# GpSimd scales expert 0's output, constant products before the gathered rows, and a reordered, halved last weight split, in a decoder layer with hierarchical MoE

## The reference, cut to what matters

```python
def hier_moe(x, w_group, b_group, w_expert, b_expert, w_gate, w_up, w_down):
    xt = x.reshape(B_ * S, D)                       # 512 x 1024
    ...
    combine = jnp.einsum('tk,tke->te', w_tok, jax.nn.one_hot(gid, N_EXPERTS, dtype=jnp.float32)).astype(x.dtype)
    y = jnp.zeros_like(xt)
    for e in range(N_EXPERTS):                      # 16
        h = jax.nn.silu(xt @ w_gate[e]) * (xt @ w_up[e])
        y = y + combine[:, e:e + 1] * (h @ w_down[e])
    return y.reshape(B_, S, D)

def reference(...):
    ...
        x = layer_norm(DEEPNORM_ALPHA * x + mix, ln1_g[l], ln1_b[l])
        moe = hier_moe(x, w_group[l], b_group[l], w_expert[l], b_expert[l], w_gate[l], w_up[l], w_down[l])
        x = layer_norm(DEEPNORM_ALPHA * x + moe, ln2_g[l], ln2_b[l])
```

## Time and profile before

| | us |
|---|---|
| median of 3 runs (663.3 to 665.82) | 664.22 |
| the profiled execution | 664.12 |
| its span, first to last instruction | 662.3 |
| TensorE busy | 619.7 (94%) |
| VectorE busy | 479.0 (72%) |
| ScalarE busy | 377.3 (57%) |
| GpSimd busy | 100.5 (15%) |
| granted TensorE clock, mean | 0.971 |

### The profile page before, as it was taken

One profiled execution on the slowest core, in us unless ns is written; L12 is line 12 of the kernel. 1 busy time (PEld: TensorE's weight loads), 2 busy tenths in 40 slices (PEclk: granted clock), 3 DMA queues, 4 the chain that ended last, 5 costly groups with the idle time before them and its releaser, 6 DMA issues.

```text
span 662.3 us, 9787 instructions
## 1 busy us (share of the span) xinstructions
PE 619.7 (94%) x3745; PEld 499.6 (75%) x3745; DVE 479.0 (72%) x554; ACT 377.3 (57%) x401; POOL 100.5 (15%) x78
## 2 busy tenths in 40 slices
PE   9998999999999999999599599999999999999990
PEld 7877788787767888887477388888888888888870
DVE  3668698884357334455778478899898898888857
ACT  4568234531306576311555478777877777878734
POOL 0023124450000000000156111101111111110000
PEclk9999999999999999999889799999999999999995
DMA  8732131125006000956589889999999999999353
GB/s 332 246 129 95 54 109 64 64 71 133 2 1 190 1 1 2 389 245 254 192 329 421 277 301 388 391 392 390 393 391 390 392 392 401 401 403 380 85 156 127
DMA packets 42413, 155.25 MB, mean 234 GB/s; under 512 B 11923, under 2 KB 12131, under 8 KB 30092
## 3 DMA queue, kind: packets, MB, share of 16 engines
q1 hardware_dynamic: 37500, 138.40, 54.1%
q0 software_dynamic: 4880, 16.39, 9.5%
HBM read 139.96 MB, written 14.81 MB: 234 GB/s over the span
## 4 chain that ended last, share of the span: by engine, by line
PE 82%; DVE 5%; ACT 4%; issue 3%; DMA 3%; POOL 2%; DVEq 0%; ACTq 0%; POOLq 0%
PE psum L618 23%; PE psum L620 21%; PE psum L619 21%; PE psum L851 3%; PE psum L627 2%; PE psum L731 2%; PE psum L1001 2%; PE psum L1018 1%; DMA slot_dram<-rec_i,addr_i 1%; PE psum L829 1%; PE psum L842 1%; PE psum L761 1%; DMA slots<-slot_dram 1%; POOL slot_dram L553 1%; DVE ring L1462 1%
## 5 line engine op out<-in xcount | busy, mean ns | idle before, releaser
L1656 DVE TENSOR_TENSOR w_lo<-ring,w_hi 128x2048 fp32r<-128x2048 f32 x96 | 218.3, 2290 | 24.5 <-ACT w_hi L1282 24.2
L618 PE MATMUL psum<-w_hi,act_hi 128*128 128x512 f32 x544 | 222.2, 408 | 12.1 <-DVE w_lo L1656 8.3
L620 PE MATMUL psum<-w_hi,act_lo 128*128 128x512 f32 x544 | 214.1, 394 | 0.0
L619 PE MATMUL psum<-w_lo,act_hi 128*128 128x512 f32 x544 | 213.9, 393 | 0.0
L1282 ACT ACTIVATE w_hi<-ring 128x2048 fp32r<-128x2048 f32 x96 | 182.0, 1916 | 25.0 <-PE psum L620 25.0
L618 PEld LDWEIGHTS psum<-w_hi,act_hi 128*128 128x128 f32 x544 | 103.3, 190 | 40.1 <-issue 12.6
L620 PEld LDWEIGHTS psum<-w_hi,act_lo 128*128 128x128 f32 x544 | 103.0, 189 | 22.4
L619 PEld LDWEIGHTS psum<-w_lo,act_hi 128*128 128x128 f32 x544 | 103.4, 190 | 19.1
L1417 DVE TENSOR_TENSOR w_lo<-ring,w_hi 128x2048 fp32r<-128x2048 f32 x17 | 41.8, 2462 | 33.6 <-ACT w_hi L1131 33.4
L579 POOL DMA_INDIRECT acc_dram<-misc,slots x15 | 23.9, 1597 | 217.9 <-ACT misc L1332 217.9
L1131 ACT ACTIVATE w_hi<-ring 128x2048 fp32r<-128x2048 f32 x17 | 32.5, 1915 | 42.7 <-PE psum L620 41.0
(11 more groups left out here) (232 smaller groups left out, 723.3 us busy)
## 6 DMA issues: line engine op xcount, KB each, us to landing
ring<-in_w_gate SPq DMA_DIRECT2D x32, 1024.0 KB, 11.9
ring<-in_w_up SPq DMA_DIRECT2D x32, 1024.0 KB, 13.9
ring<-in_w_down SPq DMA_DIRECT2D x32, 1024.0 KB, 11.5
ring<-in_w_in SPq DMA_DIRECT2D x13, 1024.0 KB, 5.4
ring<-in_w_o SPq DMA_DIRECT2D x4, 1024.0 KB, 5.0
acc_dram<-ring SPq DMA_DIRECT2D x5, 512.0 KB, 3.6
ring<-in_x SPq DMA_DIRECT2D x2, 1024.0 KB, 6.4
ring<-strip_dram SPq DMA_DIRECT2D x8, 256.0 KB, 5.0
```

The costliest lines, as they stand in the source:

```text
L618: pe.matmul(dst, lh, rh, start=first, stop=False, skip_group_check=True)
L619: pe.matmul(dst, lh, rl, start=False, stop=False, skip_group_check=True)
L620: return pe.matmul(dst, ll, rh, start=False, stop=last, skip_group_check=True)
L1656: dve.tensor_tensor(w_lo[:, v0 % WBUF, :], ring[:, slot, :], w_hi[:, v0 % WBUF, :].bitcast(F32), ALU.subtract).then_inc(s_lo, 1)
```

## The change

Three parts. **Expert 0's output.** ScalarE copies it unscaled to `yb` as soon as its down product is complete (`first_out`), without waiting for a weight. GpSimd, once the table is there, multiplies these 128x1024 numbers by the weights in place, and then scatters them. `weight_column(0)` goes; the new product counts in its place, and expert 1's output waits for one count instead of two. **Constants.** TensorE issues 24 constant matmuls into bank 1 before it waits for the first gathered rows; before the last expert's down product it issues 6 and 10 instead of 24 and 14. **The last units.** VectorE makes the last expert's gated product before the low part of unit 95 and makes that low part in two halves, the low part of the turned product between them. TensorE waits for each half where it first needs it. The column and the one-hot rows of the last expert come behind all of this on VectorE.

```diff
-            weight_column(0)
             weight_column(1)
             pool.wait_ge(s_acc, 16 * (T + 1))
+            pool.wait_ge(s_y, 1)
+            pool.tensor_scalar(yb[:, 0, :], yb[:, 0, :], weight_of(slots[:, 0, 2:3]), None, ALU.mult).then_inc(s_wnow, 1)
+            pool.wait_ge(s_wnow, 2)
             for e in range(NE - 1):
...
+            keep_warm(24, 1)
             pe.wait_ge(s_xg[0], 16)
...
-            keep_warm(24, 0)
+            keep_warm(6, 0)
             transpose_h(NE)
-            keep_warm(14, 0)
+            keep_warm(10, 0)
             pe.wait_ge(s_htlo, NE)
             pe.wait_ge(s_y, NE - 1)
-            pe.wait_ge(s_lo, MIX_UNITS + 6 * NE)
+            pe.wait_ge(s_lo, MIX_UNITS + 6 * NE - 1)
             for dhalf in range(2):
                 for c in range(4):
+                    if dhalf == 0 and c >= 2:
+                        pe.wait_ge(s_lolast, c - 1)
...
-                act.wait_ge(s_wnow, e + 1)
+                act.wait_ge(s_wnow, 1 if first else e + 1)
                 act.activation(yb[:, b, :], banks(5, 2), ACT.Copy, scale=w_now[:, b:b + 1]).then_inc(s_y, 1)
+
+            def first_out(v0):
+
+                act.wait_ge(s_used, MIX_UNITS + v0)
+                act.activation(yb[:, 0, :], banks(5, 2), ACT.Copy).then_inc(s_y, 1)
...
-                y_out(s - 1, 1 - b, v + 4, j, first=s0 <= 2)
+                if s0 == 1:
+                    first_out(v + 4)
+                else:
+                    y_out(s - 1, 1 - b, v + 4, j, first=s0 == 2)
...
-                elo(v + 7, j)
+                if ahead:
+                    elo(v + 7, j)
                 hidden(s, v + 6, j)
...
+            def last_lo(part):
+
+                v0 = 6 * NE - 1
+                cols = slice(part * D, (part + 1) * D)
+                return dve.tensor_tensor(w_lo[:, v0 % WBUF, cols], ring[:, (v0 + 3) % RING, cols],
+                                         w_hi[:, v0 % WBUF, cols].bitcast(F32), ALU.subtract)
+
+            dve.wait_ge(s_hi, MIX_UNITS + 6 * NE)
+            dve.wait_ge(s_used, MIX_UNITS + 6 * NE - WBUF)
+            last_lo(0).then_inc(s_lolast, 1)
+            dve.wait_ge(s_hthi, NE)
+            dve.tensor_tensor(h_lo, bank(4), h_hi.bitcast(F32), ALU.subtract).then_inc(s_htlo, 1)
+            last_lo(1).then_inc(s_lolast, 1)
+            dve.wait_ge(s_lolast, 2)
+            dve.sem_inc(s_lo, 1)
             dve.wait_ge(s_flag, 2)
             over = dve.value_load(over_i[0:1, 0:1], min_val=0, max_val=1)
             dve.wait_ge(s_slotd, 16)
             link(dve.tensor_copy(last_row, slots[:, NE - 1, 1:2]))
             dve.wait_ge(s_lnw, 80)
             dve.tensor_scalar(hot_last, token_no, last_row, None, ALU.is_equal).then_inc(s_onehot, 1)
-            dve.wait_ge(s_hthi, NE)
-            dve.tensor_tensor(h_lo, bank(4), h_hi.bitcast(F32), ALU.subtract).then_inc(s_htlo, 1)
```

More of the change, by code:

```diff
@@ L325, in build @@
         s_comb, s_zsum, s_nmu, s_rstd = sem("s_comb"), sem("s_zsum"), sem("s_nmu"), sem("s_rstd")
-        s_xo = sem("s_xo")
+        s_xo, s_lolast = sem("s_xo"), sem("s_lolast")
         w_in = t["w_in"].rearrange("(k p) (b n) -> p k b n", p=P, n=WIDTH)
```

## The result

The changed kernel takes 655.43 us (median of 4 runs, 654.15 to 655.68), the kernel before 663.85 us (4 runs, 663.3 to 665.82): ratio 0.9867, 95% interval 0.985 to 0.9883. The forecast was 651.3 us with a range of 648.6 to 654.8, so the direction was right and the gain, 8.4 us, is two thirds of the 12.8 forecast. The profiled execution took 655.68 us, its span is 653.9.

A forecast was written before the change was run, and what follows sets the result against it. The expert loop was taken as TensorE's, with DMA engines as full, time being winnable only at three stops or slow-clock places; from 664.1 us, -10.7 + 1.0 + 0.3 - 1.6 - 1.8 = -12.8 gave 651.3 us, range 648.6 to 654.8.

The forecast's parts named there:

- Expert 0's output, -10.7: Second expert step: without ScalarE's wait for the weight column, TensorE's hole and its slow clock go, -10.7 us.
- The weights, nothing: Weight loads, needed up to 12.3 us earlier, keep about 4 us of reserve; costed at nothing.
- The rival of weights running dry: End of the loop: TensorE waits for weight loads and gives back up to 5 us, 656 us; chance 0.05.
- VectorE held by the product, +1.0 (0 to +2.2): GpSimd's product near 368 to 370 us holds a VectorE split; about half reaches TensorE, +1.0 us.
- The gather chain, +0.3 (0 to +3): GpSimd's queue from product through two scatters to expert 4's gather: rows at about 394.8, needed at 396; +0.3 us.
- my rival on the slow side: Gather chain's end: a product of 13.7 us or more, with low clock costing 2.5 us, makes a loss; chance 0.02.
- the gather chain is late: Expert 4's rows: scatter or product longer than assumed, 1 to 4 us more, 652.5 to 655.5 us; chance 0.10.
- The constants, -1.6 (+1.5 to -2.0): Router's end: 24 constant products before the first gathered rows bring the full clock back earlier, -1.6 us.
- near 331: Router's end: with the constants starting at 327.6, the full clock may be back near 331 us instead of 337.3.
- The tail, -1.8: Last expert: gated product starts 1.9 us earlier, the load of the sums holds 0.1 back; -1.8 us, bounds -1.9 and 0.
- that rival: Tail: with fewer constant products the clock falls, 24 down matmuls cost 5.3 us more, 656.6 us; chance 0.05.

The follow-up runs named there:

- the gather ahead: Changed kernel with GpSimd issuing expert 4's gather once the slot table is there, before the product and both scatters: 650.37 us, ratio 0.979.
- the half product: Changed kernel with GpSimd's product on only the first 512 of 1024 columns of expert 0's output: 654.47 us, ratio 0.9869.
- two products: Changed kernel with GpSimd's product on expert 0's output made twice, one after the other: 658.07 us, ratio 0.9914.
- the repeat of the better kernel: Changed kernel with expert 4's gather issued before the product and both scatters, run again unchanged in a later batch: 651.17 us, ratio 0.9801.
- all gathers ahead: Kernel with expert 4's gather before product and scatters, plus gathers of experts 5 to 7 before the wait for the preceding scatter: 649.4 us, ratio 0.9787.
- the old output: Changed kernel with expert 0's output waiting for its weight column again, no GpSimd product, constants and new tail kept: 660.43 us, ratio 0.995.

## Why the forecast was right in direction and wrong in size

**Expert 0's output, -10.7.** Measured -10.8. Taking the last step of the loop as the model for the undisturbed one held to 0.1 us.

**The weights, nothing.** No high part waited for a load, and the up units, from 320 us on, took 14.1 us to land in the median. The rival of weights running dry fell.

**VectorE held by the product, +1.0 (0 to +2.2).** 0 in the changed kernel; about 0.8 with the gather ahead, where the step took 378.58 - 369.11 = 9.47 us against 8.68. Right in kind. But I had asked only what GpSimd does to VectorE. What VectorE does to GpSimd was the costly part, though the rows that I quoted had it too (3.34 us for a product of 1.48).

**The gather chain, +0.3 (0 to +3): the step that failed.** I wrote "the chain is just in time". It cost 5.2 us. TensorE's time of need was right: 396 forecast, 400.43 - 4.17 = 396.3 measured. The supply was not: 394.8 forecast, 400.4 measured. Piece by piece, forecast and measured: product begins 368.30 and 369.27 (+0.97); from there to the scatter's issue 2.20 and 5.20 (+3.00); first scatter to the second 10.10 and 11.24 (+1.14); second scatter to the gather 2.00 and 3.95 (+1.95); gather to its rows 12.20 and 10.77 (-1.43). Together +5.63 us. The +3.00 are 2.07 of waiting for a split, 0.65 for the product itself (2.85 alone, 2.2 taken) and 0.28 between product and scatter. Most of it and the +1.95 are one error: I took the durations of GpSimd's instructions from places where no split of VectorE ran beside them (its two copies took 0.31 us, and the 2.01 us from the scatter at 391.88 to the gather lie almost wholly between two splits, one that ends at 392.05 and one that starts at 394.35). In the new place VectorE splits tile after tile. That the size of the product alone would not have saved it is shown by the half product (the same chain to 0.1 us; one execution), and that the order would have, by the gather ahead of it, in two batches.

Two more faults lie in the same step. I took one value where the chain's slack, 396 - 394.8 = 1.2 us, was smaller than three of the errors of its five terms and a fifth of their sum; a chain that close should have been forecast as late. And I left the clock out of its price, though my rival on the slow side had it: a stop of 4.17 us brought 1.27 us of slow clock. The rival "the gather chain is late" gave 652.5 to 655.5 and held the median (its own terms, 651.3 plus 1 to 4, give 652.3 to 655.3, just short of it); its 0.10 was far too little, and the range stopped short of its end.

**The constants, -1.6 (+1.5 to -2.0).** Measured -1.3 at expert 2; the medians differ by 1.0 us with the rows of expert 4 late, and by nothing that can be told with the gather ahead. The 24 took 4.39 us, from 327.20 to 331.59, and so ended before the rows landed; the clock came back at 331.6, as forecast "near 331". Unforeseen: the transposes of expert 0 now waited for the rows until 332.10, half a microsecond later than before.

**The tail, -1.8.** -1.9 at the transposes, as worked out; 0.4 back at the load of the sums, forecast 0.1: -1.5. The clock kept 2.4 GHz through all matmuls of the tail (it fell at 638.8), so that rival fell too.

With the chain at +5.2, VectorE's hold at 0 and the rest as forecast the sum is 664.1 - 10.7 + 5.2 - 1.6 - 1.8 = 655.2 us, within 0.5 of the profiled execution.

## What to carry to other kernels

When a change shortens the path to a step, list what that step also needs and compare the slack of each supply with the error of its estimate; here a chain of five queued pieces with 1 us of slack was 4 us late. An instruction put into an in-order queue delays everything behind it, so put the request with the nearest due time ahead of it: one line moved gave 5 us. And take an instruction's duration from rows in which the neighbouring engine does what it will do in the new place.

## What the runs showed of the hardware that I had not expected

**GpSimd waits out VectorE's split, VectorE only a part of the product.** The 128x1 copy takes 0.19 us free and 2.35 us when it is issued as a 2.28 us split starts (368.85 and 368.88 in the kernel with the gather ahead); a scatter's own time is 1.57 us free and up to 3.38, a gather's 1.02 and up to 2.94 (with two products). The other way round a product of 2.87 us lengthened the split beside it by only 1.15 us, to 3.43, in the kernel with the gather ahead. The page "SBUF — State Buffer" of the Trainium skill ("Who interferes with whom") has these two engines exclude each other for such operands. For GpSimd the rows agree: its copies end with a split to 0.04 us, and its scatters are stretched by the same splits. For VectorE they agree where GpSimd's product has two inputs: in the kernel before, a 128x2048 one (L525) ran from 49.91 to 53.60, and the split at 51.50 took 4.26 us, so it was held about to that end. Beside the new product, which has one input tile, they don't: one begun at 369.39 ran to 372.26, and the pair of splits at 370.44 took 4.62 us, no more than a pair with GpSimd idle (4.66 at 384.68 in the kernel before); one begun at 370.46, without the constants, made the split at 370.94 take 2.77. By these two and the 3.43 us such a product holds VectorE for about its first microsecond only; that is an estimate from three rows.

**One kernel has two levels of time, by a fall of the clock far ahead of the change.** TensorE idles 1.9 us before 57.6 to 58.1 in every profile here. In some executions the granted clock then falls to 0.50 for 3.4 us, in others it doesn't. The profile of the kernel before and that without constants have no fall there, but one from about 214 to 218 us, behind an idle time of 1.35 us (before 213.70 in the kernel before) that the changed kernel has too (before 215.30), without a fall. The same stretch of two profiles, the repeat of the better kernel and the one with all gathers ahead, whose code is the same up to there:

```profile
58.60:62.60 4.00, 4.00 (x17) 3.25 (x15) 2.25 (x2) 3.06 (x4) 0.00 (x0) 0.58 0.49 187
```
```profile
58.60:62.60 4.00, 4.00 (x24) 3.38 (x23) 2.22 (x2) 3.05 (x4) 0.00 (x0) 1.00 0.37 142
```

Seven matmuls fewer were done, and the load of the slot table comes at 363.99 and at 361.61 us. The profiled times are 651.5 and 648.72. The 24 runs with the gather ahead and the constants (four kernels, one of them twice) fall into two groups: with a mean clock of 0.986 or 0.987 they took 648.3 to 649.6 us, with 0.981 to 0.985 they took 650.3 to 651.7. That the groups are those with and without a fall is read from the five profiled ones among them. The account of the change compares like with like: with a fall at 58 us after and at 214 us before, TensorE's small products at the router's end start at 326.22 and 326.29, and at 324.64 in the profile with the old output, which has neither. The profile of the changed kernel has this fall, that of half the product hasn't, which explains the latter's 1.7 us without any gain in the chain. The page "TensorE: Matmul & The Clock Gate" of the Trainium skill (Part 1, "The HAM clock gate") has the moment depend on a free-running phase; two outcomes from the same code agree with that, but no run here shows the phase itself. For work on this kernel it means that differences under 2 us are read from the rows, or between executions with the same falls.
